# Five of 96 expert weight pieces moved as transfers of 112, 8 and 8 partitions

## The reference

```
expert = chosen group * 8 + top 2 of the 8 experts in it        # for each token
y      = (silu(x @ w_gate[e]) * (x @ w_up[e])) @ w_down[e]        # w_gate_up[e]: 1024 x 1024, w_down[e]: 512 x 1024
x      = x + sum over a token's two experts of gate * y
```

## Time and profile before

| | us |
|---|---|
| median of 3 runs (lowest, highest) | 970.13 (969.71, 971.74) |
| the profiled execution: its time | 969.6 |
| its span, first to last instruction | 967.8 |
| PE (TensorE) busy in the span | 823.7 (85%) |
| DVE, ACT, POOL busy | 339.0, 190.1, 324.4 |
| chain that ended last: PE, DMA, SP's queue | 60%, 26%, 6% |

### The profile page before, as it was taken

The page is one execution under the profiler, slowest core; times in us unless marked ns, Lnnn a source line. Parts: engine busy times, 40 slices in busy tenths (PEclk is TensorE's granted clock), DMA queues, the critical chain, the costliest instruction groups (busy, mean ns, idle before and its releaser), DMA issues.

```text
span 967.8 us, 18379 instructions
## 1 busy us (share of the span) xinstructions
PE 823.7 (85%) x8064; PEld 654.6 (68%) x8064; DVE 339.0 (35%) x864; ACT 190.1 (20%) x354; POOL 324.4 (34%) x169
## 2 busy tenths in 40 slices
PE   8999999999999999999999996666756657667574
PEld 7999988889999999999887653333333323333332
DVE  2688323647263434343214352211112112121112
ACT  2521138731231000102012111011110111110102
POOL 5876630038998879996300000000000000000000
PEclk9999999999999999999999999889798798877888
DMA  9854534443564444447597999999999999999994
GB/s 311 247 180 175 174 131 159 146 150 113 175 218 174 139 162 149 166 172 270 221 428 310 412 428 427 425 429 425 428 427 427 426 427 428 425 429 426 427 424 183
DMA packets 62406, 285.32 MB, mean 295 GB/s; under 512 B 6693, under 2 KB 11641, under 8 KB 50169
## 3 DMA queue, kind: packets, MB, share of 16 engines
q1 hardware_dynamic: 58056, 280.84, 73.0%
q10 hardware_dynamic: 4272, 3.32, 1.2%
HBM read 283.08 MB, written 1.06 MB: 294 GB/s over the span
## 4 chain that ended last, share of the span: by engine, by line
PE 60%; DMA 26%; SPq 6%; DVE 2%; ACT 2%; another core or an unknown queue 1%; POOL 1%; issue 1%; ACTq 0%; DVEq 0%; POOLq 0%
PE bank L1678 31%; DMA ring<-in_w_gate_up_dram 10%; DMA blk<-in_w_gate_up_dram 10%; PE bank L1576 7%; SPq L418 6%; PE bank L1950 5%; DMA ring<-in_w_down_dram 5%; PE bank L1673 5%; PE bank L1974 2%; PE bank L1644 1%; PE bank L1916 1%; PE bank L1832 1%; PE bank L1812 1%; PE bank L1905 1%
## 5 line engine op out<-in xcount | busy, mean ns | idle before, releaser
L1678 PE MATMUL bank<-blk,ring 128*128 128x128 f32 x1840 | 213.4, 275 | 0.4 <-POOL blk L546 0.4
L1678 PEld LDWEIGHTS bank<-blk,ring 128*128 128x128 f32 x1840 | 209.3, 192 | 1.9 <-issue 1.8
L1950 PE MATMUL bank<-ring,cbm 128*32 128x256 f32 x1088 | 80.1, 444 | 43.5 <-DMA ring<-in_w_gate_up_dram 43.5
L1421 DVE TENSOR_TENSOR cbm<-bank,gq 128x256 f32<-128x256 f32 x31 | 13.2, 425 | 251.1 <-PE bank L1916 251.1
L1950 PEld LDWEIGHTS bank<-ring,cbm 128*32 128x32 f32 x1088 | 40.0, 123 | 77.1 <-issue 54.7
L1576 PE MATMUL bank<-blk,ring 128*128 128x256 f32 x384 | 85.4, 381 | 0.8 <-DVE blk L1343 0.8
L1950 PE MATMUL bank<-blk,cbm 128*32 128x256 f32 x768 | 53.7, 425 | 31.1 <-DMA blk<-in_w_gate_up_dram 31.1
L1576 PEld LDWEIGHTS bank<-blk,ring 128*128 128x128 f32 x384 | 72.1, 190 | 11.6 <-DVE blk L1343 1.2
L510 POOL TENSOR_TENSOR ring<-ring 128x1024 f32<-128x1024 f32 x20 | 47.3, 2366 | 97.1 <-DVE dec L1141 75.6
L1678 PE MATMUL bank<-ring 128*128 128x128 f32 x608 | 71.0, 275 | 0.0
L1678 PEld LDWEIGHTS bank<-ring 128*128 128x128 f32 x608 | 69.4, 192 | 0.0
(11 more groups left out here) (345 smaller groups left out, 1084.7 us busy)
## 6 DMA issues: line engine op xcount, KB each, us to landing
ring<-in_w_gate_up_dram SPq DMA_DIRECT2D x34, 2048.0 KB, 49.8
blk<-in_w_gate_up_dram SPq DMA_DIRECT2D x24, 2048.0 KB, 49.9
ring<-in_w_in_dram SPq DMA_DIRECT2D x19, 2048.0 KB, 7.9
ring<-in_w_down_dram SPq DMA_DIRECT2D x18, 2048.0 KB, 49.5
blk<-in_w_down_dram SPq DMA_DIRECT2D x10, 2048.0 KB, 50.6
params<-in_w_gate_up_dram SPq DMA_DIRECT2D x6, 2048.0 KB, 50.6
ring<-in_w_kv_dram SPq DMA_DIRECT2D x4, 2048.0 KB, 8.3
params<-in_w_down_dram SPq DMA_DIRECT2D x3, 2048.0 KB, 49.4
```

Of the source, the lines that this page charges most:

```text
L1421: v.tensor_tensor(xeN, gu_bank(p)[:, T:2 * T], gq[:, :], ALU.mult).then_inc(sem["xn3_ready"], 1)
L1678: last = mm(out_[:, f], wt[:, k, f * P:(f + 1) * P], xt[:, k, :], start=k == 0, stop=k == 3)
L1950: last = mm(gu_bank(p)[c * WIN:(c + 1) * WIN, 0:2 * SEG], xe[:, xin, 4 * j + k, :], w[:, k, :, c, :], start=4 * j + k == 0, stop=4 * j + k ...
```

## The change

`part` gets a parameter `uneven`. For the pieces k in `UNEVEN` = (20, 35, 50, 65, 80), each a `w_down` (k % 3 is 2), it makes three transfers in place of one: partitions 0 to 111, 112 to 119 and 120 to 127. Each adds 16 to the buffer's semaphore, so `fills`, from which TensorE's waits are worked out, counts two more for each such piece that a buffer has had. The overflow blocks' count is written by way of `fills`.

```diff
+    UNEVEN = (20, 35, 50, 65, 80)
+    EDGE = 16
...
     def fills(k):
         s = TURNS[k % RING]
         before = PREFILLS - (s == 0) if s < PRE else 0
-        return before + k // RING + 1
+        return before + k // RING + 1 + 2 * sum(TURNS[m % RING] == s for m in UNEVEN if m <= k)
...
-            def part(e, j, s):
+            def part(e, j, s, uneven=False):
...
-                sp.dma_start(slot(s).rearrange("p (k n) -> p k n", k=4), src).then_inc(filled[s], 16)
+                to = slot(s).rearrange("p (k n) -> p k n", k=4)
+                if not uneven:
+                    sp.dma_start(to, src).then_inc(filled[s], 16)
+                else:
+                    for a, b in ((0, P - EDGE), (P - EDGE, P - EDGE // 2), (P - EDGE // 2, P)):
+                        sp.dma_start(to[a:b], src[a:b]).then_inc(filled[s], 16)
...
-                part(k // PARTS, k % PARTS, TURNS[k % RING])
+                part(k // PARTS, k % PARTS, TURNS[k % RING], k in UNEVEN)
...
-                        lambda j: (o + ((PREFILLS - (SPARE[j] == 0) if SPARE[j] < PRE else 0) + SPARE_FILLS + 1)) * 16, False)
+                        lambda j: (o + (fills(RING * SPARE_FILLS - PARTS + j) + 1)) * 16, False)
```

## The result

The changed kernel takes 1030.64 us, the median of 4 runs (1023.96 to 1036.42), and the kernel before 969.92 us on the same chip. The ratio is 1.0622, with a 95% interval of 1.0593 to 1.0651: slower by 60.7 us where 15.4 were forecast, and 20.6 us above the end of the range. The profiled execution took 1026.2 us with a span of 1024.4, against a span of 967.8 before, so 56.6 us of the difference can be looked for in it (it was among the shorter of the four runs).

A forecast was written before the change was run, and what follows sets the result against it. Piece arrivals were taken to bound the kernel from 600 us. Five pieces at 4.30 us make 21.5, less the 6.1 lead 15.4; 969.6 + 15.4 = 985.0 for a profile, 985.5 us for the median, range 966 to 1010.

The forecast's parts named there:

- What bounds the kernel: Expert stage from 600 us: it runs at the speed at which 2 MB pieces arrive, the last ones above all.
- SP's issues and PE's counts at nothing: Ten more issues on SP, up to 8.5 us a piece, hidden by the lead; PE's waits for three increments cost nothing.
- That is 2.46 us for a transfer of eight rows: Small transfers: eight rows to neighbouring partitions queue four in line, 2.46 us a transfer.
- Seven rows an engine, and then eight rows to eight engines: Uneven pieces: 112 partitions take 4.30 us on 16 engines; each small transfer occupies at most eight engines.
- theory A: Follow-up expectation, not in the prediction: nearby partitions share one engine's worth of destination rate; 112 rows add 6.3 us in a stream.
- the seven rows collide too: Rival, large transfer: engines meet at neighbouring partitions, 4.3 us more a piece, 1007 us; no chance of its own given.
- They led by 6.1, so they end 21.5 - 6.1: Stream's end: the small transfers' engines lose 21.5 us, less their 6.1 us lead, ending 15.4 us after the present end.
- The 80 packets more on q1: Sign in the transfer view: some 80 small packets more on q1 from ten transfers, with the same MB.
- The dips at five places with the share at 1.0: Sign of queueing: GB/s below 427 at five places, some 50 us behind the pieces' issues, DMA share at 1.00.
- the longer waits: Sign of queueing: PE's waits for weights behind the five pieces grow by over 4 us each.
- The half-share stretch: Sign at the stream's end: the stretch with half of the engines busy stays or grows with queueing.
- The last gate-up half: Sign at the stream's end: the last gate-up half lands at about 966 with queueing, 947.8 without.

The follow-up runs named there:

- the first program: Program of loads only, no kernel: single transfers, then short streams with the tested transfers amid eight whole pieces; 41.92 us with none, 46.68 with 128, 54.12 with 112, 8, 8.

## Why the prediction was wrong

**What bounds the kernel: right.** The arrivals do. The time moved with the level finish of the stream and the last engine behind it: what follows the last landing changed by 1.5 us only.

**SP's issues and PE's counts at nothing: right.** The kernel with three transfers by columns measured +0.6 us, within its interval of no change.

**"That is 2.46 us for a transfer of eight rows": right.** Two take 4.93 us in the stream of the first program, and four rows take as long as eight.

**"Seven rows an engine, and then eight rows to eight engines": this step failed first.** It gave the 112 partitions "7 packets for each of 16 engines: 4.30 us", at full rate. They take 7.7 us in the stream, 3.4 more. A likely reason is the one of its rival: seven rows to an engine are cut at other places than eight, so that two engines meet at neighbouring partitions. No trace here tells which engine moved which row, so this stays an inference, and theory A, which is built on it, did not give the sizes. The prediction had this only as a rival ("the seven rows collide too", 1007 us), and priced it at 4.3 us a piece where 3.4 were measured. The kernels with 64 + 64 and 112 + 16 show that such a cut, without transfers of 8, is enough for 49 us over five pieces.

**"They led by 6.1, so they end 21.5 - 6.1": the second failure.** The sum charged the queueing to the small transfers' engines alone and let their lead pay for it. There was no such credit: at level engines an uneven piece costs 7.0 us (3.4 + 3.7 by the short streams), and piece 20 alone costs the kernel 6.1. The dips lack these microseconds of all 16 engines, and the stream with piece 80 alone ends at half share for some 5 us, no longer than before: so both eights lose; that an engine which queues at a destination also holds up the one that is writing there would explain it, and is not shown. And with the lead the price was higher, not lower: 13.8 against 7.6 us with and without instruction packets, and 12.7 us for piece 80, where the distance is largest. Why the price of one piece rises when the other eight are behind, and not when the small transfers' own are (6.6 us), was not tried.

**The size, term by term**, in the profiled executions. Small transfers, 5 x 3.7 = 18.5 us. The cut at 112, 5 x 3.4 = 17. More for engines already apart, 48.2 - 35.5 = 12.7: this is what the dips leave over, not a measurement of its own, and takes in whatever one uneven piece adds to the next. The last engine's lag, 10.1, and 1.5 less behind it. Since the last terms are remainders, the sum meets the 56.6 us by itself. The forecast had 21.5 for the first, nothing for the second, less than nothing (-6.1) for the third, and nothing for the fourth.

**What would show it.** The 80 packets more on q1 came, with the same MB. The dips at five places with the share at 1.0 came, the first some 20 us behind its piece's issue (554.93), where the prediction had 50, and the longer waits. The half-share stretch did not stay: it became one or two engines alone for over ten microseconds. The last gate-up half landed at about 1008, where 966 was forecast, and the last down weights at 1013. That the direction came out as forecast rests on the queueing of the small rows, which was right; the size did not, and in the kernels with 64 + 64 and 112 + 16 most of the loss came without those rows. What stays open is how the rows of a cut transfer meet, which engine falls last, and why its distance grows from piece to piece.

## What to carry to other kernels

In a stream that keeps all DMA engines busy, loads over all 128 partitions kept their 0.61 us a row. Each of the three cuts by partitions that were tried (112 + 8 + 8, 112 + 16, 64 + 64) slowed the engines down, and a piece of 2 MB cut so cost 6 to 13 us, though its bytes and its rows stayed the same. Cut by columns instead: into 3584, 256 and 256 columns that was free. When the DMA share is at 1.0, read GB/s beside it in slices as long as one piece: the share did not show these losses and the GB/s did. And price every part of a cut, not only the odd small one.

## What the runs showed of the hardware

- 112 partitions take longer than 128: 9.71 against 7.78 us alone, 7.7 against 4.8 in a stream. Sharing of destinations, which gave the forecast's 2.46 us, accounts for a part when it is applied to the large transfer (6.3 us by theory A in the stream), and the rest is open.
- Instruction packets of 16 KB fall on eight of the 16 engines, and each holds its engine up by some 1.5 us. A stream of whole pieces is uneven at its end from this: 9 us in a program with 50 of them, and by the same price the 6.1 us of the kernel before.
- Rows to partitions 64 to 127 in transfers of 8, behind whole pieces, took 320 to 400 ns for 5 KB, where rows to partitions 0 to 63 took 196.
- An issue of a small transfer on SP is not cheap when the queue is full, 10.4 us for the three of the second uneven piece at 616.50 in the changed kernel, yet it cost nothing with the pieces in hand (SP's timeline: start, us taken):

```profile
612.22 4.24 SPq L422 DMA_DIRECT2D blk<-in_w_gate_up_dram  x1
616.50 10.38 SPq L425 DMA_DIRECT2D ring<-in_w_down_dram  x3
626.93 1.64 SPq L422 DMA_DIRECT2D ring<-in_w_gate_up_dram  x2
```
